# Second token half's attention transposes, value products and projection moved behind the first expert queries

## The chip, the cores and the metric

The kernel runs on one core of a Trainium2 chip. Its time is the device time of one execution in microseconds (us); the profile is one execution, taken by the hardware profiler. Engines: PE (TensorE), DVE (VectorE), ACT (ScalarE), POOL (GpSimd) and SP, which only issues transfers.

## The reference, cut to what matters

Two transformer blocks run one after the other on 256 tokens of width 1024, in float32. The change touches the second block: an attention of 8 heads beside a long convolution, both gated, merged and projected, and then a retrieval layer ("peer"), in which each token picks 8 x 16 rows out of two tables of 16384 rows.

```python
    merged = (jax.nn.sigmoid(g_attn) * (attn @ p["w_attn_out"])
              + jax.nn.sigmoid(g_hy) * (hy @ p["w_hy_out"]))
    return merged @ p["w_out"], k_self, v_self
...
        x = x + g1 * out
        x = x + g2 * peer(modulate(rmsnorm(x, norm_ffn_g[i]), sh2, sc2),
                          peer_wq[i], peer_keys1[i], peer_keys2[i], peer_u[i], peer_v[i])
...
    def chunk(xc):
        q = (xc @ wq).reshape(PEER_CHUNK, PEER_HEADS, 2, half)
        s1 = jnp.einsum('chd,hnd->chn', q[:, :, 0], keys1).astype(jnp.float32)
        s2 = jnp.einsum('chd,hnd->chn', q[:, :, 1], keys2).astype(jnp.float32)
        v1, i1 = lax.top_k(s1, PEER_TOPK)
        v2, i2 = lax.top_k(s2, PEER_TOPK)
        cand = (v1[..., :, None] + v2[..., None, :]).reshape(PEER_CHUNK, PEER_HEADS, PEER_TOPK * PEER_TOPK)
...
        best, pos = lax.top_k(cand, PEER_TOPK)
        eidx = jnp.take_along_axis(cidx, pos, axis=-1)
        g = jax.nn.softmax(best, axis=-1)
        a = jnp.einsum('chkd,cd->chk', u_tab[eidx], xc)
        wgt = (jax.nn.gelu(a.astype(jnp.float32)) * g).astype(xc.dtype)
        return jnp.einsum('chk,chkd->cd', wgt, v_tab[eidx])
```

## The kernel before, in words

The instructions of every engine stand in the order in which the code lists them; there is no scheduler. Engines wait for each other on counting semaphores. The 256 tokens are two halves of 128, t = 0 and t = 1, each one token per partition.

Attention of the second block works on eight pairs of heads-and-half: pairs 0 to 3 are half 0, pairs 4 to 7 half 1. Of pair i, `score2(i)` multiplies queries and keys into two PSUM banks, DVE takes the maximum (`unit_max`), ACT the exponential (`exp_units`), DVE divides (`unit_norm`), PE transposes the probabilities (`pt2`), ACT copies the transposes out, and PE multiplies with the values (`pv2`). After pair 3 and pair 7 ACT copies a half's result into `attnT` (`pw0`, `pw1`). `mixed_half(br, t, u)` is 16 products of 128x128 of the output projection of branch br (0 attention, 1 convolution) for half t and column half u; `merge_half` on DVE multiplies it with its gate, and adds the two branches. `out_unit_rows(place2, "b", t, n)` is the projection by `w_out`, `mix_in` adds it to the residual, `pn_square` and `pn_rows` normalize it, `half_T` transposes it, and `half_out` leaves the retrieval layer's input in `actT`.

The retrieval layer: `queries(j, t)` multiplies with the j-th quarter of the query weights (64 products of 128x128; for t = 0 quarters 0 and 1 go in two parts, "a" and "b"), and `key_scores(t, j)` compares with the keys; group j covers heads 2j and 2j+1. DVE finds the best 16 of each head (`best_of`, `rows_of_table`; both for a group and one more step are `picks_of`), and writes row numbers (`rowid`, which counts `rowid_ready` up). POOL issues one indirect DMA of 128 rows x 4 KB per pick, 512 in all, in turns of 32: {u0, u1, v0, u2, v1, ...}. A u row is multiplied with the token on DVE (`dots_of`, line 2197), a v row is weighted and summed on PE (`sum_rows`, line 1044). In the text gather n is the n-th of the 512, counted from 1.

A gathered row lands in one of 28 rooms of 4 KB per partition. The first 54 gathers take rooms by the table `ROW_ORDER`, later ones the room used longest ago. A room must have been read before it is used again. Most rooms lie in weights' places that PE reads first: `room_reader` names the PSUM group after which POOL may write there. Rooms 12 to 15 come free after `queries(0, 1)` ("pq01"), 16 to 19 after "pq11", 20 to 23 after "pq21" and 24 to 27 after "pq31", the last queries. In `ROW_ORDER` of before gather 39 is the first that takes room 20, and gather 51 the first that takes room 24. POOL also waits so that no more than 6 gathers (from the 65th on 10) are under way.

## Time and profile before

| | us |
|---|---|
| median of 3 runs | 1729.56 (1727.46 to 1732.55) |
| the profiled execution, its own time | 1723.73 |
| its span, first to last instruction | 1721.9 |
| PE busy | 1456.2 (85%) |
| DVE busy | 885.1 (51%) |
| POOL busy | 503.7 (29%) |
| ACT busy | 318.5 (18%) |

The span is the time between the first and the last instruction of any engine. Times in rows count from its start. In a timeline a row merges equal instructions that follow each other; what stands in brackets is how long the engine was idle before it, and what ended that ("issue": nothing that the profile shows). The first gather is issued at 949.18 us, so the retrieval layer's gathers fill the last 45% of the span.

### The profile page before, as it was taken

The numbers are of one execution on the slowest core, as the hardware profiler recorded it, in microseconds if no ns is written. First come the engines' busy times: TensorE is split into PE (matmuls) and PEld (weight loads), VectorE is DVE, ScalarE is ACT, GpSimd is POOL, SyncE is SP. The second block draws the span as 40 slices with busy tenths as digits, with TensorE's granted clock in tenths as the row PEclk, the third lists the DMA queues.
The fourth block names the chain that finished last, engine by engine and source line by source line (L and its number), as shares of the span: only waits on it lengthen the run. The fifth ranks groups of instructions, "written<-read, shape, count | busy, mean of one in ns | idle before, by whom it ended". The sixth has DMA issues, their size and how long they took to land.

```text
span 1721.9 us, 18101 instructions
## 1 busy us (share of the span) xinstructions
PE 1456.2 (85%) x6206; PEld 804.7 (47%) x6206; DVE 885.1 (51%) x1997; ACT 318.5 (18%) x643; POOL 503.7 (29%) x541
## 2 busy tenths in 40 slices
PE   7989989999999999999999874767767685867566
PEld 6866564444443434478878663222323232322222
DVE  3975152323232323465453988492938385744744
ACT  3124231101010101301052113111202021210001
POOL 3000000000000000000000555666666757575773
PEclk9999999999999999999999986787878788888789
DMA  9779729999999999943340978999999999999996
GB/s 314 277 278 337 293 99 382 427 428 429 429 428 429 429 428 428 381 147 125 120 135 1 343 295 317 360 394 379 350 409 330 404 340 391 337 392 349 379 370 251
DMA packets 135357, 565.40 MB, mean 328 GB/s; under 512 B 11513, under 2 KB 17446, under 8 KB 122748
## 3 DMA queue, kind: packets, MB, share of 16 engines
q1 hardware_dynamic: 60668, 295.66, 43.2%
q0 software_dynamic: 74416, 268.84, 40.8%
q8 instruction: 33, 0.54, 0.1%
q14 instruction: 32, 0.26, 0.0%
q10 hardware_dynamic: 208, 0.09, 0.0%
HBM read 563.49 MB, written 1.06 MB: 328 GB/s over the span
## 4 chain that ended last, share of the span: by engine, by line
PE 76%; issue 11%; DMA 5%; DVE 4%; POOL 3%; ACT 1%; another core or an unknown queue 0%; SPq 0%; POOLq 0%; DVEq 0%; ACTq 0%
PE psum L413 52%; PE psum L1044 22%; DMA ring<-in_peer_v_dram,attnT 2%; POOL ring L1194 2%; DVE arena L1645 1%; DMA ring<-in_peer_u_dram,attnT 1%; DMA ring<-in_w_in_dram 1%; PE psum L898 0%; DMA tok<-in_peer_v_dram,attnT 0%; PE psum L768 0%; PE psum L774 0%; DMA dft<-in_peer_v_dram,attnT 0%; POOL tok L1194 0%; DVE spec L1654 0%; PE psum L662 0%
## 5 line engine op out<-in xcount | busy, mean ns | idle before, releaser
L1044 PE MATMUL psum<-ring,arena 128*128 128x512 f32 x772 | 384.1, 647 | 180.3 <-DMA ring<-in_peer_v_dram,attnT 106.1
L1044 PEld LDWEIGHTS psum<-ring,arena 128*128 128x128 f32 x772 | 156.8, 206 | 404.7 <-issue 323.2
L413 PE MATMUL psum<-ring,arena 128*64 128x512 f32 (+1 forms) x1552 | 340.4, 594 | 1.4 <-DVE arena L1885 1.4
L2197 DVE CUSTOM_DVE_ANT_0 scratch<-ring,psum 128x1024 f32<-128x1024 f32 x216 | 255.5, 1219 | 68.6 <-DMA ring<-in_peer_u_dram,attnT 57.9
L413 PE MATMUL psum<-actT,ring 128*128 128x256 f32 (+1 forms) x1424 | 268.1, 349 | 21.6 <-issue 19.8
L1194 POOL DMA_INDIRECT dft<-in_peer_u_dram,attnT x10 | 9.9, 990 | 938.8 <-DVE attnT L2167 934.0
L413 PEld LDWEIGHTS psum<-actT,ring 128*128 128x128 f32 x1424 | 237.6, 197 | 52.3 <-issue 29.3
L1194 POOL DMA_INDIRECT ring<-in_peer_u_dram,attnT x216 | 205.9, 953 | 161.0 <-issue 63.9
L1194 POOL DMA_INDIRECT ring<-in_peer_v_dram,attnT x218 | 209.5, 961 | 70.1 <-issue 61.9
L413 PEld LDWEIGHTS psum<-ring,arena 128*64 128x64 f32 (+1 forms) x1552 | 109.2, 137 | 217.2 <-issue 203.8
L1495 ACT ACTIVATE arena<-ident,attnT 128x128 f32<-128x128 f32 x226 | 81.8, 396 | 412.5 <-PE psum L1044 183.6
L1927 DVE TENSOR_TENSOR arena<-arena,psum 128x512 f32<-128x512 f32 x16 | 16.9, 1058 | 203.9 <-PE psum L413 203.9
L413 PEld LDWEIGHTS psum<-arena,scratch 128*128 128x128 f32 x544 | 63.3, 192 | 13.3 <-issue 13.3
L413 PE MATMUL psum<-arena,scratch 128*128 128x128 f32 x544 | 67.8, 278 | 0.0
L413 PE MATMUL psum<-tok,arena 128*128 128x512 f32 x128 | 59.2, 605 | 0.0
L413 PE MATMUL psum<-ring,tok 128*128 128x512 f32 x128 | 55.8, 594 | 1.6 <-DVE tok L1753 1.6
L1951 DVE TENSOR_TENSOR resid<-resid,psum 128x512 f32<-128x512 f32 x64 | 44.0, 687 | 13.9 <-PE psum L413 13.9
L2230 DVE SCALAR_TENSOR_TENSOR scratch<-ring,attnT,scratch 128x1024 f32<-128x1024 f32 x24 | 30.8, 1285 | 37.9 <-DMA ring<-in_peer_v_dram,attnT 22.8
L1945 DVE COPY tok<-psum 128x512 f32<-128x512 f32 x16 | 11.1, 692 | 72.9 <-PE psum L413 72.9
L1645 DVE SCALAR_TENSOR_TENSOR arena<-arena,colsB 128x256 f32<-128x256 f32 x120 | 47.7, 480 | 0.0
L2122 DVE MAX8 qT<-arena 128x8 f32<-128x128 f32 x64 | 16.7, 288 | 57.4 <-remote 36.3
L1388 ACT ACTIVATE arena<-psum 128x512 f32<-128x512 f32 x16 | 9.6, 597 | 182.8 <-PE psum L413 182.8
(404 smaller groups left out, 1368.3 us busy)
## 6 DMA issues: line engine op xcount, KB each, us to landing
ring<-in_w_gate_dram SPq DMA_DIRECT2D x32, 2048.0 KB, 12.3
ring<-in_w_up_dram SPq DMA_DIRECT2D x32, 2048.0 KB, 16.5
ring<-in_w_down_dram SPq DMA_DIRECT2D x32, 2048.0 KB, 13.7
ring<-in_w_in_dram SPq DMA_DIRECT2D x15, 2048.0 KB, 14.7
ring<-in_ada_w_dram SPq DMA_DIRECT2D x12, 2048.0 KB, 11.7
ring<-in_w_out_dram SPq DMA_DIRECT2D x4, 2048.0 KB, 9.0
ring<-in_peer_wq_dram SPq DMA_DIRECT2D x4, 2048.0 KB, 15.1
ring<-in_w_attn_out_dram SPq DMA_DIRECT2D x2, 2048.0 KB, 11.8
```

The source lines that it names most:

```text
L413: return nc.tensor.matmul(o, lhsT, rhs, start=(k == 0), stop=(k == n - 1))
L1044: last = nc.tensor.matmul(psum[:, 4 + 2 * t + n, :], diag[:, i, :], rowbufs[b][:, n * 512:(n + 1) * 512], start=first, stop=final)
L1194: pool.indirect_dma_start(out=rowbufs[b], out_offset=None, in_=tab, in_offset=bass.IndirectOffsetOnAxis(ap=rowid[:, j // 4, k:k + 1], axis ...
L1388: nc.scalar.activation(silu, psum[0:BOTH, 3, :], ACT.Silu).then_inc(ev("silu_ready"), 1)
L1495: nc.scalar.activation(diag[:, i, :], ident[:, :], ACT.Identity, scale=gates[:, j // 4, k:k + 1]).then_inc(ev("diag_ready"), 1)
L1645: V.scalar_tensor_tensor(yT[:, c, :], vpad[:, c, j:j + T], w, yT[:, c, :], ALU.mult, ALU.add).then_inc(ev("tap"), 1)
L1927: V.tensor_tensor(hperm, silu.rearrange("p (q k) -> p q k", k=4), psum[0:BOTH, 4, :].rearrange("p (q k) -> p q k", k=4), ALU.mult).then_in ...
L1945: V.tensor_copy(yrow[:, 512:1024], psum[0:BOTH, 6, :]).then_inc(ev("y_ready1"), 1)
L1951: V.tensor_tensor(r, r, psum[:, MIX_BANK[n, t], :], ALU.add).then_inc(ev("mixed"), 1)
L2122: step(V.max(vals[:, 8 * r:8 * r + 8], src))
L2197: V.tensor_tensor_reduce(dotjunk[:, i % junk, :], rowbufs[b], x, 1.0, 0.0, ALU.mult, ALU.add, dots[:, t, k:k + 1]).then_inc(ev("dotted"), 1)
L2230: V.scalar_tensor_tensor(acc, rowbufs[b], w, acc, ALU.mult, ALU.add).then_inc(ev("added"), 1)
```

## The change

In the eight-pair loop only half 0 is finished. Scores and softmax of pairs 6 and 7 are placed around the attention projection of half 0, and `pt2`, `pv2` of pairs 4 to 7 and both attention projections of half 1 (`mixed_half(0, 1, 0)` and `(0, 1, 1)`) now stand behind `queries(0, 0, "a")`. The convolution's projection of half 1, which was spread over the loop, takes the place that the attention's had. Probabilities get a room for each pair instead of four in turn. The output projection of half 1 stands behind all queries of groups 0 and 1 of half 0, and on DVE `picks_of(1)` before `mix_in(1, 0)`. Rooms 2 to 5 and 6 to 9 trade their places in memory, and the table of rooms is a new one; gather 43 is now the first that takes room 20, and gather 51 still the first that takes room 24.

PE, from the end of the attention loop to the output projection of half 0. L898 are the probabilities' transposes, `scratch,vtok` the value products, `kdup,qT` the scores, `attnT,ring` the attention projection, `ring,tok` the output projection. Before:

```order
L898 MATMUL psum<-ident,arena 128x128 x8
L413 MATMUL psum<-scratch,vtok 64x128 x8
L413 MATMUL psum<-kdup,qT 128x512 x2
L898 MATMUL psum<-ident,arena 128x128 x8
L413 MATMUL psum<-scratch,vtok 64x128 x8
L413 MATMUL psum<-attnT,ring 128x128 x16
L898 MATMUL psum<-ident,arena 128x128 x8
L413 MATMUL psum<-scratch,vtok 64x128 x8
L413 MATMUL psum<-attnT,ring 128x128 x16
L898 MATMUL psum<-ident,arena 128x128 x8
L413 MATMUL psum<-scratch,vtok 64x128 x16
L413 MATMUL psum<-ring,tok 128x512 x16
```

The same place in the changed kernel, from the last transposes of half 0 on:

```order
L899 MATMUL psum<-ident,arena 128x128 x8
L414 MATMUL psum<-scratch,vtok 64x128 x16
L414 MATMUL psum<-kdup,qT 128x512 x2
L414 MATMUL psum<-attnT,ring 128x128 x32
L414 MATMUL psum<-kdup,qT 128x512 x2
L414 MATMUL psum<-ring,tok 128x512 x16
L414 MATMUL psum<-arena,ring 128x128 x16
L962 MATMUL psum<-ident,arena 128x128 x16
L422 MATMUL psum<-ident,scratch 128x128 x8
```

The transposes and value products of half 1 are gone from here; two scores stand between and behind the projections.

PE, behind the first key scores (`spec,arena`; `actT,ring` are queries, `arena,ring` the convolution's projection). Before:

```order
L413 MATMUL psum<-spec,arena 128x128 x2
L413 MATMUL psum<-actT,ring 128x128 x16
L413 MATMUL psum<-arena,ring 128x128 x16
L413 MATMUL psum<-spec,arena 128x128 x2
L413 MATMUL psum<-actT,ring 128x128 x16
L413 MATMUL psum<-ring,tok 128x512 x16
L413 MATMUL psum<-actT,ring 128x128 x16
L413 MATMUL psum<-spec,arena 128x128 x4
L421 MATMUL psum<-ident,scratch 128x128 x8
L413 MATMUL psum<-actT,ring 128x128 x32
```

The changed kernel, from the second query part on (eight transposes stand ahead of it):

```order
L414 MATMUL psum<-actT,ring 128x128 x16
L414 MATMUL psum<-scratch,vtok 64x128 x8
L899 MATMUL psum<-ident,arena 128x128 x8
L414 MATMUL psum<-spec,arena 128x128 x2
L414 MATMUL psum<-scratch,vtok 64x128 x8
L899 MATMUL psum<-ident,arena 128x128 x8
L414 MATMUL psum<-scratch,vtok 64x128 x8
L899 MATMUL psum<-ident,arena 128x128 x8
L414 MATMUL psum<-scratch,vtok 64x128 x8
L414 MATMUL psum<-attnT,ring 128x128 x32
L414 MATMUL psum<-actT,ring 128x128 x32
L414 MATMUL psum<-spec,arena 128x128 x4
```

The output projection of half 1 and its transposes now come behind these rows, and nothing stands between them.

POOL, gathers 15 to 23 of before. `tok` are rooms 10 and 11, `dotted` counts rows that DVE has read, `row_in` rows that have landed, and `bank_full` a PSUM bank that PE has filled, here "bx11" (the output projection of half 1) and "pq01":

```order
L1194 DMA tok<-in_peer_u_dram,attnT 128x1024 [waits row_in8,bank_full6]
L1194 DMA tok<-in_peer_u_dram,attnT 128x1024 [waits row_in9]
L1194 DMA ring<-in_peer_u_dram,attnT 128x1024 [waits row_in0,dotted,rowid_ready]
L1194 DMA ring<-in_peer_u_dram,attnT 128x1024 [waits row_in1,dotted]
L1194 DMA ring<-in_peer_u_dram,attnT 128x1024 [waits row_in2,dotted]
L1194 DMA ring<-in_peer_u_dram,attnT 128x1024 [waits row_in3,dotted]
L1194 DMA ring<-in_peer_u_dram,attnT 128x1024 [waits row_in10,bank_full5]
```

Gathers 17 to 23 of the changed kernel, where bank 3 is that of "bx11":

```order
L1200 DMA ring<-in_peer_u_dram,attnT 128x1024 [waits row_in0,dotted,rowid_ready]
L1200 DMA tok<-in_peer_u_dram,attnT 128x1024 [waits row_in1,bank_full3]
L1200 DMA tok<-in_peer_u_dram,attnT 128x1024 [waits row_in2]
L1200 DMA ring<-in_peer_u_dram,attnT 128x1024 [waits row_in3,dotted]
L1200 DMA ring<-in_peer_u_dram,attnT 128x1024 [waits row_in4,dotted]
L1200 DMA ring<-in_peer_u_dram,attnT 128x1024 [waits row_in5,dotted]
L1200 DMA ring<-in_peer_u_dram,attnT 128x1024 [waits row_in6,bank_full5]
```

The wait for "bx11" moved from gather 15 to gather 18, and that for "pq01" from gather 21 to gather 23.

```diff
@@ -198,7 +198,9 @@
...
-prob2 = arena2[:, 2048:4096].rearrange("p (u c) -> p u c", c=512)
+prob_rooms = [arena2[:, 0:1024], arena2[:, 1024:2048], arena2[:, 2048:3072], arena2[:, 3072:4096],
+          arena1[:, 3072:4096], arena2[:, 1024:2048], arena2[:, 2048:3072], arena2[:, 3072:4096]]
+prob2 = [room[:, 512 * r:512 * (r + 1)] for room in prob_rooms for r in range(2)]
...
@@ -217,25 +219,24 @@
...
-vflat = vtok[:, :, :].rearrange("p c t -> p (c t)")
...
-wi = vflat[:, 0:256].bitcast(U32).rearrange("p (t n) -> p t n", t=NT)
-wf = vflat[:, 256:512].rearrange("p (t n) -> p t n", t=NT)
+wi = rel[:, 0:64].bitcast(U32).rearrange("p (t n) -> p t n", t=NT)
+wf = rel[:, 64:128].rearrange("p (t n) -> p t n", t=NT)
...
-rowbufs += [ring[:, 4, r * D:(r + 1) * D] for r in range(4)] + [ring[:, 0, r * D:(r + 1) * D] for r in range(4)]
+rowbufs += [ring[:, 0, r * D:(r + 1) * D] for r in range(4)] + [ring[:, 4, r * D:(r + 1) * D] for r in range(4)]
...
-ROW_ORDER = [*range(10), *range(4), 10, 11, *range(4, 8), *range(12, 20), *range(8, 12), *range(0, 6), *range(20, 24), *range(6, 10), *range(12, 16), *range(24, 28)]
+ROW_ORDER = [*range(10), *range(7), 10, 11, *range(7, 10), *range(12, 20), *range(7), 10, 11, *range(7, 10), *range(20, 24), *range(12, 16), *range(24, 28)]
...
@@ -936,36 +937,32 @@
...
 mixed_half(1, 0, 1, (7,))
-for i in range(len(pairs)):
-    if i + 2 < len(pairs):
-        score2(i + 2)
+for i in range(4):
+    score2(i + 2)
     pt2(i)
...
         pv2(i - 1)
-    if i < 4:
-        mixed_half(1, 1, 0, (6,), (i,))
-    if i == 5:
-        landed(place2, "o0")
-        emptied(pe, "pw0")
-        mixed_half(0, 0, 0, (6,))
-    if i == 6:
-        mixed_half(0, 0, 1, (0,))
-pv2(len(pairs) - 1)
-everyday.append((7, 1, 2, 3, 4, 5, 6, 0))
+pv2(3)
+score2(6)
+landed(place2, "o0")
+emptied(pe, "pw0")
+mixed_half(0, 0, 0, (6,))
+mixed_half(0, 0, 1, (7,))
+score2(7)
+everyday.append((5, 4))
 pe.wait_ge(ev("bmerged"), 1)
...
 out_unit_rows(place2, "b", 0, 1)
-emptied(pe, "pw1")
-mixed_half(0, 1, 0)
+mixed_half(1, 1, 0, (6,))
 pe.wait_ge(ev("keys_in"), 32)
...
 for g in range(4):
-    b = bank(f"keyT{g}")
+    b = bank(f"keyT{g}", (3, 0, 1, 2))
     for c in range(4):
...
 half_T("pn", scratch, "pn_ready", 0)
-mixed_half(0, 1, 1)
+mixed_half(1, 1, 1, (7,))
 everyday.append((2, 3, 4, 5, 6, 7))
...
@@ -1004,15 +1001,24 @@
...
 key_scores(0, 0, "a", (0, 1), ("a",))
+pt2(4)
 queries(0, 0, "b", (2, 3))
-mixed_half(1, 1, 1)
+pv2(4)
+pt2(5)
 key_scores(0, 0, "b", (2, 3), ("b",))
+pv2(5)
+for i in (6, 7):
+    pt2(i)
+    pv2(i)
+emptied(pe, "pw1")
+mixed_half(0, 1, 0)
+mixed_half(0, 1, 1)
 queries(1, 0, "a", (0, 1))
+queries(1, 0, "b", (2, 3))
+key_scores(0, 1, need=("a", "b"))
 pe.wait_ge(ev("bmerged"), 2)
...
 out_unit_rows(place2, "b", 1, 1)
-queries(1, 0, "b", (2, 3))
-key_scores(0, 1, need=("a", "b"))
 half_T("pn", scratch, "pn_ready", 1)
...
@@ -1175,7 +1181,7 @@
...
-room_reader = {2: "bo011", 6: "bo111", 10: "bx11", 12: "pq01", 16: "pq11", 20: "pq21", 24: "pq31"}
+room_reader = {2: "bo111", 6: "bo011", 10: "bx11", 12: "pq01", 16: "pq11", 20: "pq21", 24: "pq31"}
...
@@ -1418,11 +1424,11 @@
...
-        if u >= 4:
-            full(act, f"qt{u - 4}")
+        if u >= 10:
+            full(act, f"qt{u - 8}")
...
-        last(nc.scalar.activation(prob2[:, u % 4, :], full(act, f"sc{u}"), ACT.Exp, bias=stat("nm2", 16)[:, u:u + 1], scale=HD ** -0.5,
+        last(nc.scalar.activation(prob2[u], full(act, f"sc{u}"), ACT.Exp, bias=stat("nm2", 16)[:, u:u + 1], scale=HD ** -0.5,
...
@@ -1447,15 +1453,18 @@
...
-exp_units(0)
-for i in range(HEADS):
-    if i + 1 < HEADS:
-        exp_units(i + 1)
+def prob_out(i):
...
-    if i == 4:
-        copy_out("pw0", attnT[:, :, 0:P])
-copy_out("pw1", attnT[:, :, P:T])
+
+exp_units(0)
+for i in range(4):
+    exp_units(i + 1)
+    prob_out(i)
+copy_out("pw0", attnT[:, :, 0:P])
+exp_units(5)
+exp_units(6)
+exp_units(7)
...
@@ -1500,12 +1509,17 @@
...
 scores_out(0, 0, "a", 0, 2)
+prob_out(4)
 queries_out(0, 0, "b", 2, 2)
+prob_out(5)
 scores_out(0, 0, "b", 2, 2)
+prob_out(6)
+prob_out(7)
+copy_out("pw1", attnT[:, :, P:T])
 queries_out(1, 0, "a", 0, 2)
-pn_square(1)
 queries_out(1, 0, "b", 2, 2)
 scores_out(0, 1)
+pn_square(1)
 half_out("pn", 1, modsc[:, 2, :], mod[:, 24:32, 0])
...
@@ -2083,17 +2097,19 @@
...
 merge_half(1, 0, 0)
-for i in range(HEADS):
+for i in range(4):
     unit_norm(i)
...
         merge_half(1, 0, 1)
-    if i + 2 < HEADS:
-        unit_max(i + 2)
-    if i == 3:
-        merge_half(1, 1, 0)
-    if i == 6:
-        merge_half(0, 0, 0, True)
+    unit_max(i + 2)
+unit_norm(4)
+unit_max(6)
+merge_half(0, 0, 0, True)
 merge_half(0, 0, 1, True)
+unit_norm(5)
+unit_max(7)
+unit_norm(6)
+unit_norm(7)
 dve.wait_ge(ev("g1_in"), 16)
...
@@ -2110,9 +2126,9 @@
...
 pn_rows(0)
-merge_half(0, 1, 0, True)
+merge_half(1, 1, 0)
 half_out("pn", 0, modsc[:, 2, :], mod[:, 24:32, 0])
-merge_half(0, 1, 1)
+merge_half(1, 1, 1)
 
...
@@ -2252,19 +2268,22 @@
...
 rows_of_table(0, (0,))
-merge_half(1, 1, 1, True)
 best_of(0, (1,), "0b")
...
 shift_of(0)
+full(dve, "pw1")
+dots_of(0, range(0, 3), 1)
+merge_half(0, 1, 0, True)
+merge_half(0, 1, 1, True)
+dots_of(0, range(3, 7), 1)
+picks_of(1)
 mix_in(1, 0)
-dots_of(0, range(0, 4), 1)
 mix_in(1, 1)
-dots_of(0, range(4, 5), 1)
+dots_of(0, range(7, 9), 1)
 pn_rows(1)
-dots_of(0, range(5, 8), 1)
+dots_of(0, range(9, 11), 1)
 half_out("pn", 1, modsc[:, 2, :], mod[:, 24:32, 0])
-picks_of(1)
-dots_of(0, range(8, GROUP))
+dots_of(0, range(11, GROUP))
 weigh(0)
...
```

## Rows read from the trace of the kernel before

**Rows 1.** The page, part 2: busy tenths of the DMA engines in 40 slices.

```profile
DMA  9779729999999999943340978999999999999996
```

**Rows 2.** Timeline of PE, 875 to 912: start, us, engine, line, shapes, count.

```profile
875.82 1.13 PE L413 MATMUL psum<-kdup,qT 64*128 64x512 f32 x4
...
876.88 1.09 PE L898 MATMUL psum<-ident,arena 128*128 128x128 f32 x8
...
877.81 1.06 PE L413 MATMUL psum<-arena,ring 128*128 128x128 f32 x8
...
880.88 1.09 PE L413 MATMUL psum<-scratch,vtok 128*64 128x128 f32 x16
...
898.27 3.84 PE L413 MATMUL psum<-attnT,ring 128*128 128x128 f32 x32
...
910.71 14.00 PE L413 MATMUL psum<-ring,tok 128*128 128x512 f32 x32
```

**Rows 3.** Timeline of PE, 938 to 976 us.

```profile
938.78 0.68 PE L413 MATMUL psum<-spec,arena 128*128 128x128 f32 x4
...
950.46 13.95 PE L413 MATMUL psum<-ring,tok 128*128 128x512 f32 x32
...
964.25 3.73 PE L413 MATMUL psum<-actT,ring 128*128 128x128 f32 x32
...
975.71 9.01 PE L413 MATMUL psum<-actT,ring 128*128 128x128 f32 x64 [3.92 <-issue]
```

**Rows 4.** Timeline of PE, 985 to 1047 us.

```profile
985.43 15.02 PE L413 MATMUL psum<-actT,ring 128*128 128x128 f32 x131
...
1012.79 8.19 PE L413 MATMUL psum<-actT,ring 128*128 128x128 f32 x51 [0.35 <-issue]
...
1020.82 1.06 PE L413 MATMUL psum<-spec,arena 128*128 128x128 f32 x8
...
1021.71 7.20 PE L413 MATMUL psum<-actT,ring 128*128 128x128 f32 x63
...
1038.18 8.26 PE L413 MATMUL psum<-actT,ring 128*128 128x128 f32 x58 [0.33 <-issue]
...
1046.27 4.63 PE L413 MATMUL psum<-spec,arena 128*128 128x128 f32 x40
```

**Rows 5.** Timeline of POOL: gathers 1, 25, 38, 39, 50, 51 and 92.

```profile
949.18 1.03 POOL L1194 DMA_INDIRECT dft<-in_peer_u_dram,attnT  x1 [934.03 <-DVE attnT L2167]
...
993.02 0.94 POOL L1194 DMA_INDIRECT ring<-in_peer_u_dram,attnT  x1 [3.02 <-PE psum L413]
...
1009.20 0.95 POOL L1194 DMA_INDIRECT ring<-in_peer_u_dram,attnT  x1 [0.30 <-issue]
...
1021.25 0.93 POOL L1194 DMA_INDIRECT ring<-in_peer_u_dram,attnT  x1 [11.11 <-PE psum L413]
...
1035.08 0.93 POOL L1194 DMA_INDIRECT ring<-in_peer_u_dram,attnT  x1 [0.30 <-issue]
...
1046.71 0.94 POOL L1194 DMA_INDIRECT ring<-in_peer_u_dram,attnT  x1 [10.69 <-PE psum L413]
...
1097.75 0.94 POOL L1194 DMA_INDIRECT ring<-in_peer_v_dram,attnT  x1 [0.31 <-issue]
```

**Rows 6.** Timeline of ACT, 880 to 933 us.

```profile
880.61 1.23 ACT L1234 ACTIVATE scratch<-psum 128x512 f32<-128x512 f32 x2
```

**Rows 7.** Timeline of DVE, 966 to 1093 us.

```profile
966.29 0.69 DVE L2101 TENSOR_TENSOR scratch<-spec,psum 128x512 f32<-128x512 f32 x1
...
975.65 0.49 DVE L2122 MAX8 qT<-arena 128x8 f32<-128x128 f32 x2
...
990.03 0.18 DVE L2167 CAST attnT<-attnT 128x32 int32<-128x32 f32 x1
...
1044.95 1.22 DVE L2197 CUSTOM_DVE_ANT_0 scratch<-dft,psum 128x1024 f32<-128x1024 f32 x1
...
1091.64 1.22 DVE L2197 CUSTOM_DVE_ANT_0 scratch<-ring,psum 128x1024 f32<-128x1024 f32 x1 [0.89 <-issue]
```

More of the change, by code:

```diff
@@ L897, in pt2 @@
                     for kc in range(4):
-                        last = nc.tensor.transpose(psum[:, b, kc * P:(kc + 1) * P], prob2[:, u % 4, kc * P:(kc + 1) * P], ident[:, :])
+                        last = nc.tensor.transpose(psum[:, b, kc * P:(kc + 1) * P], prob2[u][:, kc * P:(kc + 1) * P], ident[:, :])
                     last.then_inc(bank_full[b], 1)
@@ L2024, in unit_norm @@
                 for u in (2 * i, 2 * i + 1):
-                    v(V.tensor_scalar(prob2[:, u % 4, :], prob2[:, u % 4, :], stat("m2", 16)[:, u:u + 1], None, ALU.mult), "p2_ready")
+                    v(V.tensor_scalar(prob2[u], prob2[u], stat("m2", 16)[:, u:u + 1], None, ALU.mult), "p2_ready")
             half_ = lambda ap: ap.rearrange("p k c -> p (k c)")
@@ L2163, in rows_of_table @@
                 for half, op, arg in halves:
-                    v_pair(V.tensor_reduce(wf[:, half, ns], hot[half].rearrange("p (n a) -> p n a", a=PTOP), AX.X, ALU.add))
+                    v_pair(V.tensor_reduce(wf[:, half, 0:n], hot[half].rearrange("p (n a) -> p n a", a=PTOP), AX.X, ALU.add))
                 v_done()
-                v(V.scalar_tensor_tensor(rowf[:, t, ns], wf[:, 0, ns], float(PKEYS), wf[:, 1, ns], ALU.mult, ALU.add))
+                v(V.scalar_tensor_tensor(rowf[:, t, ns], wf[:, 0, 0:n], float(PKEYS), wf[:, 1, 0:n], ALU.mult, ALU.add))
                 v(V.tensor_copy(rowid[:, t, ns], rowf[:, t, ns]), "rowid_ready")
```

6 lines of the change are left out of this document (3 added, 3 removed).

## Prediction, made before the changed kernel ran

> **What bounds the kernel now.** I read the page first. Its DMA row [rows 1] shows slices of 9 tenths in most of the tail, so from the first gather on the kernel moves table rows almost without a pause, 512 gathers of 512 KB. The question is what holds POOL, which issues them. Its timeline [rows 5] has three numbers that matter. Gather 1 waits 934 us for the row numbers. Gathers 39 and 51 then wait 11.1 and 10.7 us for PE: they need rooms that the query weights occupy until PE has used them ("pq21", "pq31"). From gather 51 at 1046.7 on no wait for query weights is left. The tail behind it, 1721.9 - 1046.7 = 675.2 us, consists of turns that depend on each other (rooms, dots, sums), so I take it as rigid: it starts when gather 51 does. Not gather 1 but the last query product sets the end.
>
> That makes PE's path up to "pq31" the one to follow. PE is without a gap from 875.8 to 910.7 [rows 2], then projection, first queries, first key scores, which end at 939.3 [rows 3]; queries of half 1 start at 975.7 [rows 3], the first block of key scores of group 2 at 1020.8, and the last at 1046.3 [rows 4]. Within the last part PE stands nearly still twice: the block of 131 products ends at 1000.45 and the next dense one starts at 1012.79, and again from 1028.9 (1021.71 + 7.20) to 1038.18 [rows 4]. In both stretches gathers run in a chain (13 steps from 993.02 to 1009.20, 1.245 us each), and PE comes back 3.6 and 3.1 us after the last issue of the chain (1009.20, 1035.08) [rows 4, 5]. The trace names no cause; I call it the stall under gathers, and price it by these rows.
>
> **Step 1, the first gather.** What leaves PE's way ahead of the output projection of half 0: four `pt2` at 1.03, four `pv2` at 1.03 and the four interleaved quarters of the convolution's projection at about 1.0 each, 12.2 us [rows 2]; later both kernels have two half projections ahead of the first key scores. New waits: the second pair's transposes wait for its maximum and division, which the interleaved quarter hid (0.5), and nothing but one score pair of 1.06 covers the merge of the last projection, two DVE passes of 0.7 [rows 7] and the hand-over (0.5); with the 0.5 that before already waited gone again, the net is about 0.5. So -11.7: the first key scores end at 927.6, gather 1 goes out at 937.5. Bounds: -12.7 (no new wait) and -9 (ACT, whose copies take 1.23 for two [rows 6] and stand in one queue with the exponentials, falls behind PE's 3.1 per pair by 0.9 each).
>
> **Step 2, from there to the queries of half 1.** Before it took 975.7 - 939.3 = 36.4 us. Moved in: four `pt2` and four `pv2`, 8.2 us, and two attention half projections where one convolution half projection stood, +3.6. That is 11.8. Waits: each `pv2` needs ACT's copies of its transposes, 0.6 each after PE has filled the bank [rows 6]. Query and score products cover pair 4; pair 5 shows about 0.5, pairs 6 and 7 about 1.0 each, the copy of "pw1" 0.9, a bank that ACT must first read 0.5, the key scores of group 1 0.5: 4.4. Last, the residual and norm of half 1. Before, PE had the last query part and key scores (4.6 us) to do while DVE and ACT worked between the end of the output projection at 964.25 and 975.71 [rows 3]. Now nothing is left. From the projection's end DVE needs 1.6 for the end of `picks_of(1)` and then `mix_in` twice, four passes of 0.7 (2.9); ACT a square and a root, DVE behind it the scaling, held up by two dots of 1.22 that stand ahead [rows 7] (an estimate of 3.5 for the three); PE its transposes (0.9), and DVE two more dots and its `half_out` (3.1 past the transposes): 12.0 in place of 11.5 - 4.6, so +5.1. Sum 11.8 + 4.4 + 5.1 = 21.3. Queries of half 1 start at 975.7 - 11.7 + 21.3 = 985.3, 9.6 us later than before. Bounds: +4 (half of the waits hidden) to +13 (each copy late by another 0.5, the norm by 1).
>
> `picks_of(1)` in front of `mix_in` takes 14.6 us (975.65 to 990.2) [rows 7] and needs the key scores of group 1, at about 960; it ends at 975, just behind the output projection (973.3). It costs 1.6, counted above.
>
> **Step 3, the gathers in the meantime.** Gathers 1 to 6 go out from 937.5. Gather 7 needs "bo011", now the second attention projection at 950.6; gathers 7 to 17 follow until 964. Gather 18 needs "bx11" at 973.3, gathers 20 to 22 rooms that are read behind the norm (984), gather 23 "pq01" at 994.3 (before, gather 21 needed it). From 1002.7 ("pq11" for gather 27) they run in a chain at 1.245 us until gather 42, issued at 1021.4. So 11.7 us of head start are gone: at 1009.2 before had issued 38 gathers [rows 5], now it will be about 32.
>
> **Step 4, the stall under gathers.** PE reaches the place where it stood still before (24.7 us after the start of the queries) at 1010.0. The chain has then run for 7 us, as before (993.0 to 1000.4). I let it stand until 3.6 us after gather 42, 1025.0, and add the 8.0 us of the dense rest [rows 4]: "pq21" at 1033.0, against 1020.8, +12.2. Only eight gathers (43 to 50) follow instead of twelve, the last at 1042.0; PE would reach the second standstill at 1041.1 and leaves it at 1045.1, 4.0 instead of 9.3 us; + 8.1 gives "pq31" at 1053.2, against 1046.3: **+6.9**. Bounds of both stalls together: nothing at all (then the queries end at 1035.4 and gather 51 goes 11.3 earlier than before), and as long as before, 12.4 and 9.3 (+9.5), or 15 and 9.3 (+12.2). I take +6.9, since the coupling "until the chain ends" fits both stalls within 0.5 us.
>
> By the Trainium skill, Runtime: NRT & Kernel Launch, section Instruction fetch mechanics, the next block of instructions is fetched over a DMA queue while the present one runs, and the cost of crossing a block is mostly hidden. If PE's standstill were a fetch, that rule would leave nothing to it, and this change would then be faster, as in rival A. The trace disagrees with a hidden cost, if it is a fetch: 12.3 us [rows 4]; that it is one, no row here shows.
>
> **The other queue.** DVE's dots of turn 1 start at 1044.95, after `picks_of(2)`, which needs group 2's key scores [rows 4, 7]. With "pq21" at +12.2 they start at about 1056.7, +11.8. The last of them, 1091.64 before, frees a room for gather 92 at 1097.75 [rows 5, 7]; slack 4.9, which is 11.8 - 6.9. It is a tie, and I add 0 (bounds 0 and 3). Everything else moved is covered: `wi`/`wf` in other memory, and the rooms for probabilities, change no instruction's size. Query weights 2 and 3 are loaded behind the output projection, from about 966 and 973, on a DMA queue with few gathers, and are first read at 1002.
>
> **The sum.** -11.7 + 21.3 - 2.7 (stalls) = +6.9 on the profiled execution: 1723.7 + 6.9 = 1730.6. That execution was 5.8 below the median of the runs, so for the median 1729.56 + 6.9 = 1736.5 us. Runs differ by 5.1 us among themselves; 0.3% (5.2 us) is about what can be told from no change here.
>
> **Rivals.**
>
> A, faster: PE doesn't stand still, or little. The gathers run apart for most of the stretch from 965 to 1002, so that a backlog need not build. Then gather 51 follows POOL's own pace, and the tail starts up to 11.3 earlier: 1718 us. The same time comes out if, against [rows 5], the end follows gather 1 (-11.7). For it: the first gathers, and the DMA load, do move forward. Against it: POOL waited twice for the query weights, not for row numbers. It decides if the stalls sum to less than about 8 us (before 21.7). Chance 27%.
>
> B, no change: the stalls shrink by some 5 to 10 us more than I count, or the tail absorbs the delay in pauses of its own. 1730 us. Against it: a pause of POOL ends on a room or a row, and these move along. Chance 28%.
>
> C, slower by more: `picks_of(2)` and the dots get late by more than POOL, or PE's clock stays at its lower level after the idle 973 to 985. The 64 products after 975.71 took 9.01 us where 131 took 15.02 [rows 3, 4], which is 0.026 us more each; twice as long at that pace costs 2, the dots 3: 1742 us. Chance 12%.
>
> My forecast has 33%. Slower by over 0.3%: 33 + 12 = 45%; within 0.3%: 28%; faster: 27%. The range of 8 in 10 reaches from 1717, inside A, to 1744; that of the likeliest case alone is 1732 to 1742.
>
> **What would show it.** In the profile after: gather 1 near 937 (step 1); queries of half 1 starting near 985 with an idle PE of about 8 us before their transposes (step 2); POOL waiting at gathers 7, 18 and 23 (step 3); gather 43 near 1033 and gather 51 near 1054, each after a wait for PE, and PE thin between 1010 and 1025 (step 4); and 675 us from gather 51 to the end (rigid tail). Gather 51 before 1046.7, or a tail shorter than 670, makes the forecast wrong.

## The result, and the profile after

The changed kernel takes 1750.97 us (median of 4 runs, 1749.37 to 1757.92); the kernel before, run beside it, 1729.49. The ratio is 1.0127, 95% interval 1.0106 to 1.0147: slower by 21.5 us, where +6.9 was predicted, and outside the range. The direction was the forecast's (45%). The size is three times the forecast's, and larger than rival C's (1742).

The profiled execution is the slowest of the four (1757.92, span 1756.1). In it everything is 3.7 us late already ahead of the change: the score products that started at 875.82 before [rows 2] start at 879.56. "Net" below means with that taken off. These rows of PE answer to [rows 2, 3].

```profile
930.64 0.68 PE L414 MATMUL psum<-spec,arena 128*128 128x128 f32 x4
...
947.71 1.98 PE L414 MATMUL psum<-scratch,vtok 128*64 128x128 f32 x16 [2.90 <-ACT scratch L1240]
950.62 9.05 PE L414 MATMUL psum<-attnT,ring 128*128 128x128 f32 x64 [0.93 <-ACT attnT L1240]
959.50 7.31 PE L414 MATMUL psum<-actT,ring 128*128 128x128 f32 x64
976.32 2.05 PE L414 MATMUL psum<-spec,arena 128*128 128x128 f32 x8 [9.51 <-issue]
978.16 15.51 PE L414 MATMUL psum<-ring,tok 128*128 128x512 f32 x32
1000.22 1.97 PE L422 MATMUL psum<-ident,scratch 128*128 128x128 f32 x8 [6.55 <-DVE scratch L2124]
1004.30 9.48 PE L414 MATMUL psum<-actT,ring 128*128 128x128 f32 x64 [2.11 <-DVE actT L1606]
```

The first key scores have moved from 938.78 to 930.64, the queries of half 1 from 975.71 [rows 3] to 1004.30. Between them stand three gaps: 2.90 ahead of the last value products, 9.51 ahead of the key scores of group 1, 6.55 ahead of the norm's transposes. ACT's timeline has the reason of the second.

```profile
963.33 0.38 ACT L1240 ACTIVATE arena<-psum 128x256 f32<-128x256 f32 x1 [12.77 <-PE psum L414]
975.84 0.38 ACT L1240 ACTIVATE arena<-psum 128x256 f32<-128x256 f32 x1 [12.12 <-remote]
978.46 0.60 ACT L1240 ACTIVATE arena<-psum 128x512 f32<-128x512 f32 x1 [2.24 <-PE psum L414]
```

The first row is the copy of query part "a", due 3.4 us into the chain of gathers that starts at 959.93, and prompt. The middle row is the copy of part "b". PE had its products done at 966.81 (959.50 + 7.31), 6.9 us into the chain; ACT had nothing else to do, and yet it started 9 us later. DVE then makes its picks. They end with the projection (978.16 + 15.51 = 993.67), and `mix_in` starts behind both:

```profile
979.19 0.49 DVE L2138 MAX8 qT<-arena 128x8 f32<-128x128 f32 x2 [12.96 <-ACT arena L1240]
...
993.29 0.18 DVE L2183 CAST attnT<-attnT 128x32 int32<-128x32 f32 x1
...
993.74 0.69 DVE L2117 TENSOR_TENSOR scratch<-spec,psum 128x512 f32<-128x512 f32 x1
```

The rest of PE's path answers to [rows 4].

```profile
1014.49 15.24 PE L414 MATMUL psum<-actT,ring 128*128 128x128 f32 x135
...
1044.86 7.56 PE L414 MATMUL psum<-actT,ring 128*128 128x128 f32 x46 [0.63 <-issue]
1052.26 1.06 PE L414 MATMUL psum<-spec,arena 128*128 128x128 f32 x8
...
1064.20 10.00 PE L414 MATMUL psum<-actT,ring 128*128 128x128 f32 x62 [0.16 <-issue]
1074.03 4.63 PE L414 MATMUL psum<-spec,arena 128*128 128x128 f32 x40
```

And POOL, gathers 1, 7, 17, 18, 42, 43, 50 and 51, to [rows 5].

```profile
941.05 1.03 POOL L1200 DMA_INDIRECT dft<-in_peer_u_dram,attnT  x1 [925.77 <-DVE attnT L2183]
...
959.93 0.94 POOL L1200 DMA_INDIRECT ring<-in_peer_u_dram,attnT  x1 [11.47 <-PE psum L414]
...
972.42 0.94 POOL L1200 DMA_INDIRECT ring<-in_peer_u_dram,attnT  x1 [0.30 <-DMA idft<-in_peer_u_dram,attnT]
993.94 0.94 POOL L1200 DMA_INDIRECT tok<-in_peer_u_dram,attnT  x1 [20.58 <-PE psum L414]
...
1042.03 0.94 POOL L1200 DMA_INDIRECT ring<-in_peer_u_dram,attnT  x1 [1.43 <-issue]
1052.69 0.95 POOL L1200 DMA_INDIRECT ring<-in_peer_u_dram,attnT  x1 [9.73 <-PE psum L414]
...
1061.42 0.95 POOL L1200 DMA_INDIRECT ring<-in_peer_u_dram,attnT  x1 [0.30 <-issue]
1074.47 0.94 POOL L1200 DMA_INDIRECT ring<-in_peer_u_dram,attnT  x1 [12.09 <-PE psum L414]
```

Gather 1 is 8.1 us earlier than before, gather 7 3.0 later, gather 18 16.6 later, gather 51 27.8 later; the span is 34.2 longer. Gathers 7 to 17 leave in a chain from 959.93 to 972.42, and ACT's late copy comes 3.4 us after the last of them. After its chains before, PE came back in 3.6 and 3.1 us [rows 4, 5]. In the two repeats of the changed kernel, and with the norm first on DVE (below), the copy comes 3.3 to 3.5 us after gather 17.

### The profile page after: what moved, and what is told of

Read it like the earlier page. It is cut to its first block and busy times, and to the rows that moved or that the text cites. A ratio compares the mean times of both kernels' runs of the same rounds, so it can differ in the third digit from the quotient of the medians.

```text
span 1756.1 us, 18101 instructions
## 1 busy us (share of the span) xinstructions
PE 1464.6 (83%) x6206; PEld 812.5 (46%) x6206; DVE 884.1 (50%) x1997; ACT 317.9 (18%) x643; POOL 502.4 (29%) x541
## 5 line engine op out<-in xcount | busy, mean ns | idle before, releaser
L1050 PE MATMUL psum<-ring,arena 128*128 128x512 f32 x780 | 388.7, 645 | 214.1 <-DMA ring<-in_peer_v_dram,attnT 106.1
L414 PE MATMUL psum<-actT,ring 128*128 128x256 f32 (+1 forms) x1424 | 272.2, 353 | 17.5 <-issue 13.8
L414 PEld LDWEIGHTS psum<-actT,ring 128*128 128x128 f32 x1424 | 241.3, 200 | 48.5 <-issue 24.7
L1659 DVE SCALAR_TENSOR_TENSOR arena<-arena,colsB 128x256 f32<-128x256 f32 x120 | 47.7, 485 | 0.0
L1240 ACT ACTIVATE arena<-psum 128x512 f32<-128x512 f32 (+1 forms) x33 | 18.4, 559 | 149.0 <-PE psum L414 98.6
```

The source lines that it names most:

```text
L414: return nc.tensor.matmul(o, lhsT, rhs, start=(k == 0), stop=(k == n - 1))
L1050: last = nc.tensor.matmul(psum[:, 4 + 2 * t + n, :], diag[:, i, :], rowbufs[b][:, n * 512:(n + 1) * 512], start=first, stop=final)
L1240: last(nc.scalar.activation(dst, full(act, name)[:, 0:w], func, **kw), name)
L1659: V.scalar_tensor_tensor(yT[:, c, :], vpad[:, c, j:j + T], w, yT[:, c, :], ALU.mult, ALU.add).then_inc(ev("tap"), 1)
```

## The experiments

Each ratio is against the kernel before, run beside it. The kernels ran in groups, each group on one chip. The groups fall into two kinds. In kind 1 the kernel before takes 1724 to 1729 us, as above; in kind 2 1650. In kind 2 PE does not stand still under the gathers, and 384 gathers from the 65th on take 494.4 us (the kernel with both waits out) where the kernel before took 548.5 in kind 1.

Versions of the kernel before agree in both kinds up to the queries of half 1. Versions of the changed one do not: PE's gap ahead of the last value products is 2.7 to 2.9 us in all six of kind 1 and 1.03 in all six of kind 2, and with gather 7 held the queries of half 1 start at 1001.2 in kind 1 and at 990.9 in kind 2. So a ratio of one kind says little of the other. The changed kernel itself ran in kind 1 only, where its two repeats gave 1.0128 and 1.0116; that it loses in kind 2 too is not shown. "Before, again" is 3.2 us late as a whole, from the first key scores on at the latest.

The table has all profiled runs (us; "tail" is the span less the issue of gather 51).

| kernel | kind | ratio (95%) | queries half 1 | gather 51 | tail |
|---|---|---|---|---|---|
| before (the profile ahead) | 1 | 1 | 975.7 | 1046.7 | 675.2 |
| before, again | 1 | 0.9989 (0.9974-1.0004) | 979.3 | 1051.4 | 676.2 |
| changed | 1 | 1.0127 (1.0106-1.0147) | 1004.3 | 1074.5 | 681.6 |
| changed, again | 1 | 1.0128 (1.0108-1.0149) | 1005.7 | 1076.1 | 679.4 |
| changed, third | 1 | 1.0116 (1.0099-1.0133) | 1001.6 | 1069.9 | 672.1 |
| changed, norm first on DVE | 1 | 1.0148 (1.0123-1.0172) | 1004.5 | 1076.3 | 675.7 |
| changed, gather 7 held | 1 | 1.0116 (1.0099-1.0133) | 1001.2 | 1070.9 | 673.6 |
| changed, order of before | 1 | 1.0003 (0.999-1.0015) | 981.8 | 1049.4 | 671.5 |
| before, u1 dots early | 1 | 1.0042 (1.0025-1.0058) | 975.3 | 1026.1 | 701.2 |
| before, two pauses | 1 | 0.9957 (0.9938-0.9976) | 975.5 | 1039.4 | 671.9 |
| changed, order of before | 2 | 0.9998 (0.9986-1.001) | 979.4 | 1027.2 | 618.9 |
| changed, both waits out | 2 | 1.0025 (1.0015-1.0036) | 982.9 | 1031.8 | 618.7 |
| changed, gather 7 held | 2 | 1.0079 (1.0063-1.0095) | 990.9 | 1039.7 | 619.0 |
| changed, PE's order of before | 2 | 1.0117 (1.01-1.0134) | 1000.2 | 1049.0 | 619.8 |
| changed, order of before, three pauses | 2 | 1.0015 (1.0003-1.0027) | 984.6 | 1035.8 | 618.5 |
| the same, again | 2 | 1.0015 (1.0003-1.0027) | 979.5 | 1031.5 | 619.4 |
| before, gather 1 held | 2 | 1.0049 (1.0036-1.0062) | 983.8 | 1034.7 | 619.3 |
| before, three pauses | 2 | 1.0032 (1.0021-1.0044) | 975.2 | 1032.0 | 618.5 |
| the same, again | 2 | 1.0019 (1.0007-1.0031) | 975.4 | 1032.2 | 618.7 |
| before, 3 gathers under way | 2 | 1.0192 (1.0176-1.0208) | 975.4 | 1052.1 | 626.6 |

In kind 2 the tail is 618.5 to 619.8 in all kernels but the last, while gather 51 moves by 22 us: the end follows gather 51, whatever is ahead of it. In kind 1 it is 671.5 to 681.6 but for one kernel. What gather 51 waits for can differ: with the order of before in kind 2 it goes out with an idle time of 0.34 us ahead of it, and no wait for PE.

**Both orders back.** The changed kernel, with before's order around the output projection of half 1 on three engines; the rest of the change stays.

```diff
             queries(1, 0, "a", (0, 1))
-            queries(1, 0, "b", (2, 3))
-            key_scores(0, 1, need=("a", "b"))
             pe.wait_ge(ev("bmerged"), 2)
             out_unit_rows(place2, "b", 1, 0)
             out_unit_rows(place2, "b", 1, 1)
+            queries(1, 0, "b", (2, 3))
+            key_scores(0, 1, need=("a", "b"))
...
             queries_out(1, 0, "a", 0, 2)
+            pn_square(1)
             queries_out(1, 0, "b", 2, 2)
             scores_out(0, 1)
-            pn_square(1)
...
-            picks_of(1)
             mix_in(1, 0)
...
             half_out("pn", 1, modsc[:, 2, :], mod[:, 24:32, 0])
+            picks_of(1)
```

> The changed kernel, with the order around the output projection of half 1 as in the kernel before: on PE the projection in front of the second query part and the key scores of group 1, on DVE mix_in, the norm and half_out in front of picks_of(1), on ACT the square in front of the second query part's copy. Theory: the missing cover and the stalled copy cost together about 17 us; queries of half 1 should start some 15 to 18 us earlier than in the changed kernel and the time be 1733 to 1738, above the kernel before by the uncovered waits of the attention's second half. Rival (the attention work moved behind the queries is itself what costs, or the new table of rooms): 1747 or more.

> The changed kernel with the order of before around the output projection of the second half: TensorE does it between the two parts of the second product-key queries, ScalarE's square pass stands between the two copies, VectorE mixes and norms the half before it makes its picks. All the rest of the change stays. Theory (the loss sits in the lost cover: the hand-off of query part b falls under the chained gathers with nothing behind it on TensorE, and the norm then waits behind the picks): queries of the second half start by 985, gather 51 by 1055, time 1729 to 1738. Rival (the loss sits in TensorE's own standstill or in the later value products, whatever the order): still 1745 to 1752.

Measured 0.9998 in kind 2 and 1.0003 in kind 1, where the changed kernel itself took 1.0116 in the same group: the whole loss goes with the order. I had expected 1733 to 1738 us, 1.002 to 1.005 of before; it came out better. In kind 1:

```profile
958.65 13.90 PE L414 MATMUL psum<-ring,tok 128*128 128x512 f32 x32
972.39 3.73 PE L414 MATMUL psum<-actT,ring 128*128 128x128 f32 x32
976.88 1.13 PE L414 MATMUL psum<-spec,arena 128*128 128x128 f32 x8 [0.76 <-issue]
...
981.78 7.38 PE L414 MATMUL psum<-actT,ring 128*128 128x128 f32 x64 [2.90 <-DVE actT L1606]
```

The chain of gathers runs here too (7 to 17, 955.5 to 968.4), but PE is in its projection, which takes 13.90 us as in kind 2, and ACT's copy is due only at 976, when the chain is over. Nor is there a gain: gather 1 goes out at 936.91, 12 us earlier than before [rows 5], and gather 51 at 1049.4, where PE's last queries let it.

**The copy out of the gathers' way.** GpSimd waits ahead of gather 7 until ACT has copied part "b".

```diff
+                    if turn * GROUP + i == 6:
+                        emptied(pool, "pq10b")
```

> The changed kernel with one more wait: POOL issues gather 7 only when ACT has copied out the second part of group 1's queries. Theory: in the changed kernel ACT's copy of that part came about 9 us after PE had filled the bank, because the chain of gathers 7 to 17 (959.9 to 972.4) slowed ACT, as chains slowed PE later; PE then stood idle for 9.51 us. With the chain held back the copy should follow the products within 1 us, the output projection of half 1 start some 8 to 9 us earlier, gather 51 too, and the time fall from 1751 to about 1742, although gather 7 goes out later. Rival: the copy was late for another reason (an order on ACT), or the end follows the early gathers; then the time stays at 1751 or rises by the 7 us that gather 7 is late.

> The changed kernel in which GpSimd holds gather 7 until ScalarE has copied query part b, so that no gather is under way at that hand-off. Theory (ScalarE's copy came late only because of the chained gathers 7 to 17): the 9.5 us gap of TensorE ahead of the key scores goes to 2 or less, the output projection ends by 984, but the norm still waits for the picks, so queries at 991 to 996 and gather 51 some 8 to 12 us earlier than in the changed kernel, time 1739 to 1745. Rival (the gap has another cause, and the order of gathers has no part in it): the gap stays, time 1751 or more.

In kind 1 the gap ahead of the key scores goes: 0.58, where the changed kernel of the same group has 9.31. So it was the gathers that made ACT's copy late; whether they held ACT itself or PE's signal to it, the trace does not say. It brings no time, 1.0116 as the changed kernel beside it:

```profile
964.81 1.13 PE L414 MATMUL psum<-spec,arena 128*128 128x128 f32 x8 [0.58 <-issue]
965.77 13.90 PE L414 MATMUL psum<-ring,tok 128*128 128x512 f32 x32
997.12 1.97 PE L422 MATMUL psum<-ident,scratch 128*128 128x128 f32 x8 [17.45 <-DVE scratch L2126]
```

DVE has the reason:

```profile
970.38 1.22 DVE L2215 CUSTOM_DVE_ANT_0 scratch<-ring,psum 128x1024 f32<-128x1024 f32 x1 [7.99 <-DMA ring<-in_peer_u_dram,attnT]
...
971.70 0.49 DVE L2140 MAX8 qT<-arena 128x8 f32<-128x128 f32 x2
...
990.20 0.18 DVE L2185 CAST attnT<-attnT 128x32 int32<-128x32 f32 x1
```

The projection ends at 979.7, 11.3 us ahead of the changed kernel's of this group, and PE then waits 17.45 for DVE. DVE's dots ahead of the picks want gather 7, the held one (8.0 us), and the picks, 14.6 us elsewhere, take 18.9 there, with waits of their own under the same chain. The 8.0 are the experiment's own doing: without them alone the picks would end at about 982.6 (an estimate, 990.6 - 8.0), near the projection. In kind 2, under the same chain of eleven gathers, the picks take 14.6 us, and the ratio is 1.0079 with 7.1 us of the same own doing in it. So this run shows what made the copy late, and not what the copy costs.

**The norm ahead of the picks, on DVE alone.**

```diff
-            picks_of(1)
             mix_in(1, 0)
 ...
             half_out("pn", 1, modsc[:, 2, :], mod[:, 24:32, 0])
+            picks_of(1)
```

> The changed kernel with one part of the covering order alone: on DVE mix_in, norm and half_out of half 1 in front of picks_of(1); PE's and ACT's order as in the changed kernel. Theory: where ACT's copy is late, key scores of group 1 and with them picks_of(1) are late, and this order takes picks_of(1) out of the chain to the norm; the gain is what is left of it behind the end of the output projection: 0 to 3 us on a chip without a stall, up to 2 us with the stall seen in the changed kernel (there picks_of(1) and the projection ended within 0.1 us of each other). The rest of the gap to the full covering order stays with PE's order. Rival: DVE's order is the whole cause; then this version is as fast as the full covering order.

1.0148, no gain (the changed kernel in the same group 1.0128). The copy is late as in the changed kernel (gap 9.47), PE's projection ends at 995.2, and the queries start at 1004.47: the late copy holds them by way of PE alone.

**Both at once**, gather 8 held and the norm first, PE's order as changed.

> The changed kernel with two edits: GpSimd holds gather 8 until ScalarE has copied query part b (gather 7, which VectorE's dots ahead of the picks need, is let through), and VectorE mixes and norms the second half before its picks, as before. TensorE's order stays as changed. Theory (two waits in series made the loss: the copy caught under the gathers, and the norm behind the picks): the output projection ends by 981, queries of the second half start by 990, gather 51 by 1060, time 1729 to 1737 where the changed kernel takes 1744 to 1752. Rival (TensorE's order by itself costs the time, for no cover is left for the hand-off and the norm): queries after 998, time within 3 of the changed kernel.

It fell in kind 2: 1.0025, queries at 982.94.

```profile
958.85 1.13 PE L414 MATMUL psum<-spec,arena 128*128 128x128 f32 x8 [0.58 <-issue]
959.81 13.90 PE L414 MATMUL psum<-ring,tok 128*128 128x512 f32 x32
978.86 1.97 PE L422 MATMUL psum<-ident,scratch 128*128 128x128 f32 x8 [5.15 <-DVE scratch L2126]
982.94 9.33 PE L414 MATMUL psum<-actT,ring 128*128 128x128 f32 x64 [2.11 <-DVE actT L1608]
...
992.98 21.60 PE L414 MATMUL psum<-actT,ring 128*128 128x128 f32 x192
```

With PE's order as changed, little is lost: against "order of before" in this kind the queries are 3.6 us later, the norm without cover. The changed kernel has no run in kind 2, so how much of its own loss the two edits take away is not measured; against "gather 7 held" (1.0079) they gain 8 us at the queries.

**PE's order alone put back.**

> The changed kernel with one edit: TensorE does the output projection of the second half between the two parts of the second product-key queries, as before. ScalarE and VectorE keep the changed order. Theory (each of the two waits is enough to lose the time): the projection ends by 975, but the norm still stands behind the picks, which start with the key scores at 977 to 979 and take 14.4, so queries at 999 to 1003, time within 3 of the changed kernel. Rival (TensorE's order is the cause): queries by 988, time 1724 to 1732.

1.0117 in kind 2, queries at 1000.19: PE's projection is done by 969.0, and its transposes wait for DVE, whose picks stand ahead of the norm.

```profile
996.11 1.97 PE L422 MATMUL psum<-ident,scratch 128*128 128x128 f32 x8 [21.85 <-DVE scratch L2124]
```

The copy is prompt here (0.58 ahead of the key scores), but part "b" is multiplied only behind the projection, so the picks start at 975.1. In the changed kernel the two late things are branches, not a series, and both start at the copy of part "b": copy, key scores, projection on PE, and copy, key scores, picks on DVE. PE's branch alone holds the queries at 1004 (norm first on DVE, kind 1). DVE's branch, with the picks late for either reason, is enough too (1000.2 here).

**The kernel before, gather 1 held** until the second attention projection.

```diff
+                    if turn * GROUP + i == 0:
+                        full(pool, "bx10")
```

> The kernel before with one more wait: gather 1 is issued only when PE has finished the first half of the output projection of half 1 (bx10), about 8 us later than before. Theory: the end follows gather 51, which waits for PE's last queries, so the time stays within 3 us of 1729.5. Rival: the end follows gather 1; then about 1737.5.

Gather 1 at 958.07, ratio 1.0049, 7.5 us by the medians. I had expected no cost, and the number is the rival's (8 us); but the tail is as in the other kernels, and the way is not the rival's. PE waits 9.97 us ahead of the key scores, though this is kind 2. The cause is another than in the changed kernel: DVE's first four dots stand between the two passes of `mix_in` and wait for the late rows (5.5 us for the first), ACT's square waits for `mix_in`, and the copy of part "b" stands behind the square. In this kernel gather 1 has little room to be later, though none of its being earlier pays.

**Fewer gathers under way** (3 in place of 6 for the first 64), the kernel before.

> The kernel before with at most 3 instead of 6 of the first 64 gathers under way. Theory of the stall: engines stand nearly still while a backlog of gathers is queued, so with half of it PE's standstill of 12.3 us before pq21 and 9.3 us before pq31 should shrink to half or vanish, gather 51 go out 5 to 20 us earlier, and the time fall to 1710 to 1724, unless three are too few to keep the transfers going. Rival: the standstill has to do with the rate of the transfers, not with their number in the queue; then it stays, and the time is 1729 or a few us above.

1.0192. The gathers themselves are slow then, 1.3 to 2.6 us apart, and gather 51 goes at 1052.1. In kind 2 there is no standstill that it could cure, so what I expected of the standstill was not tested.

**Dots of turn 1 earlier, rooms in another order**, the kernel before: gather 53 is the first to need "pq21", gather 67 the first to need "pq31".

> The kernel before with the gate at gather 51 taken away: DVE takes the dots of turn 1 in front of picks_of(2), and the table of rooms sends gathers 39 to 66 to rooms that DVE has read, so that the room of pq21 is first needed at gather 53 and that of pq31 at gather 67. Theory: the waits of 11.1 and 10.7 us for PE in front of gathers 39 and 51 shrink, and since the tail follows the 65th gather the time falls by 5 to 20 us. Rival: the waits move elsewhere (v rows fill all rooms until PE is done with the queries and starts summing, or weights come late); then it stays within 5 us, or is slower.

Gather 51 goes 20.6 us earlier, and the time is 1.0042: the tail is 701.2, since the wait for "pq31" now stands behind it. What it shows of the standstill is worth more: 28 gathers in one chain (993.48 to 1027.35), and PE thin from 1000.5 to 1033.05, all that time.

```profile
985.89 14.57 PE L413 MATMUL psum<-actT,ring 128*128 128x128 f32 x129
1000.68 0.36 PE L413 MATMUL psum<-actT,ring 128*128 128x128 f32 x1 [0.22 <-issue]
...
1019.73 0.37 PE L413 MATMUL psum<-actT,ring 128*128 128x128 f32 x1 [2.43 <-issue]
...
1033.05 8.24 PE L413 MATMUL psum<-actT,ring 128*128 128x128 f32 x48 [0.35 <-issue]
```

**Pauses in the chain**, the kernel before. Gather 30 waits until PE has done half of queries 2 of half 1, gather 39 for half of queries 3 of half 0 (and, with three pauses, gather 43 for half of queries 3 of half 1).

```diff
+                    if i == 1 and (j, t) in ((2, 1), (3, 0)):
+                        last.then_inc(ev("gap"), 1)
...
+                    if turn * GROUP + i == 29:
+                        pool.wait_ge(ev("gap"), 1)
+                    if turn * GROUP + i == 38:
+                        pool.wait_ge(ev("gap"), 2)
```

> The kernel before with two pauses in the chain of gathers: gather 30 waits until TensorE has done half of the unit of queries before it would run dry (queries 2 of the second half), gather 39 until it has done half of the unit after it (queries 3 of the first half). Theory (under a chain of gathers TensorE gets no new instructions, and a pause of some 3 us lets them in): the two stretches of single products shrink from 12 and 9 us to 5 or less together beyond the pauses, gather 51 is issued at 1033 to 1042 instead of 1046.7, time 1716 to 1726. Rival (the standstill is not a matter of the chain being unbroken, or returns at once after each pause): gather 51 comes at 1047 or later, time 1730 to 1740.

0.9957 (0.9938 to 0.9976), the one kernel here that is faster than before: 1714.31 beside 1724.2, in one group of kind 1. Gather 51 came where I expected it (1033 to 1042), but the thin stretches left, which I had put at 5 us together, are 12.5.

```profile
985.96 21.61 PE L413 MATMUL psum<-actT,ring 128*128 128x128 f32 x192
1007.41 1.06 PE L413 MATMUL psum<-spec,arena 128*128 128x128 f32 x8
1008.31 4.02 PE L413 MATMUL psum<-actT,ring 128*128 128x128 f32 x32
...
1016.28 10.00 PE L413 MATMUL psum<-actT,ring 128*128 128x128 f32 x65 [1.73 <-issue]
...
1034.90 4.20 PE L413 MATMUL psum<-actT,ring 128*128 128x128 f32 x21 [0.82 <-issue]
```

```profile
998.52 0.94 POOL L1200 DMA_INDIRECT ring<-in_peer_u_dram,attnT  x1 [0.30 <-issue]
1004.28 0.94 POOL L1200 DMA_INDIRECT ring<-in_peer_u_dram,attnT  x1 [4.82 <-PE psum L413]
...
1017.95 0.95 POOL L1200 DMA_INDIRECT ring<-in_peer_u_dram,attnT  x1 [2.76 <-issue]
...
1039.38 0.95 POOL L1200 DMA_INDIRECT ring<-in_peer_u_dram,attnT  x1 [6.78 <-PE psum L413]
```

The 12.3 us of standstill [rows 4] are gone with a pause of 4.8: 192 products in 21.61 us, as in kind 2. Later stretches of 3.9 and 8.6 us are left, each under the next chain. Gather 51 goes 7.3 us earlier.

**Three pauses**, on the kernel before and on the changed one with the order of before, were to take the last stretch away. Both groups that had them were of kind 2, where there is none.

> The kernel before with three pauses: gather 30 waits for half of queries 2 of the second half, gather 39 for half of queries 3 of the first half, gather 43 for half of queries 3 of the second half. With two pauses TensorE still stood 8.4 us from 1026.5 to 1034.9. Theory (a pause of about 3 us at gather 43 lets the instructions in): gather 51 at 1034 to 1037 instead of 1039.4, time 3 to 5 us under that with two pauses (0.993 to 0.995 of before). Rival (the third pause costs what it gives): ratio 0.995 to 0.998.

> The changed kernel with the order of before around the second half's output projection, and three pauses: gather 32 waits for half of queries 2 of the second half, gather 39 for half of queries 3 of the first half, gather 45 for half of queries 3 of the second half. Theory (the change itself is worth nothing, since the gathers end up waiting for TensorE's later queries, and the pauses lift the standstill): gather 51 at 1035 to 1039, ratio 0.992 to 0.996, the same as the kernel before with pauses. Rival (the earlier first gathers do pay once the standstill is gone, since fewer gathers are then left for later): ratio under 0.991.

1.0032 and 1.0015 in the first, 1.0019 (1.0007 to 1.0031) and 1.0015 (1.0003 to 1.0027) in the second: where PE does not stand still, pauses cost 2 to 5 us. What three of them bring in kind 1 was not measured, nor whether the change is worth something there once the order and the standstill are both out of the way. An unchanged copy of before gave 0.9989 (0.9974 to 1.0004), which is how far a ratio of 1 strays.

## Why the prediction was wrong, step by step

**What bounds** was right: gather 51 starts the tail, and a gather 1 that is 12 us earlier is worth nothing (1.0003 with the order of before). The tail is less rigid in kind 1 than I took it: 681.6, 679.4 and 672.1 in the changed kernel's three profiles, for 675.2.

**Step 1** was right: the first key scores net 11.9 us earlier, predicted 11.7.

**Step 2 failed.** The queries of half 1 moved by +28.6, net +24.9, where +9.6 was predicted; 15.3 us are missing. The term that failed is a wait of PE for a copy by ACT, which the step priced at what it takes when no gathers run: "the key scores of group 1 0.5". That wait took 9.51 (9.0 of the 15.3). In the same class are the last value products (2.90 for 1.0, ACT's copy of their transposes being 1.59 <-remote) and PE's slower pace behind the gaps: 9.05 for two attention half projections, where 64 such products take 7.4, 15.51 for the projection, where it took 13.95, and 2.05 for the key scores, which before PE did in about 1.1: 1.9 + 1.6 + 1.6 + 0.9. From 950 to 1000 us the mean granted clock is 0.84, where it was 0.97 before. The chain behind the projection was well estimated, 10.6 for 12.0. That is 9.0 + 6.0 - 1.4 = 13.6 of 15.3; 1.7 I can't place. The gap and its place repeat in the two other runs of the changed kernel (9.51 and 9.31). I had seen the gathers' effect in the trace and charged it to PE alone, since only PE had work there before. The change put hand-offs on ACT, and picks on DVE, into the gathers' time, and step 3 of my own working had gathers 7 to 17 going out until 964, over the copy that I priced at 0.5.

The second error hides behind the first. I took `picks_of(1)` to end just behind the projection. It does (993.7 and 993.67), but only because both hang on the same late copy. So taking the picks alone off the norm's path brought nothing; holding gather 7 alone brought nothing either, there with 8.0 us of its own. Both at once was not measured in kind 1, so that the two together are the whole loss there is argued; that the loss is the order's is shown.

**Step 3** was right in its places: POOL waits at gathers 7, 18 and 23, and at 27, 43 and 51.

**Step 4** was right, counted from the queries: "pq21" 48.0 us later (predicted 47.7), "pq31" 21.8 behind it (20.2). PE came back 2.8 us after each chain's last issue. Over the profiles of before, changed, two pauses and dots early, PE turns thin 7.0 to 8.3 us after a chain's first gather, and is back 2.0 to 3.9 us after its last, once 5.7. One bound was added up wrongly: with no stall at all the step gives 9.6 - 21.7 = -12.1 for gather 51, not -11.3, and rival A's time moves by as little. The trace can now say more of what the standstill is not. The instruction packets of one queue, in 2 us windows of the kernel with two pauses, at 1004 and at 1020 us:

```profile
q8 instruction: 1, 0.02, 2.9%
...
q8 instruction: 1, 0.02, 3.0%
```

None comes between 1022 and 1042, though PE is thin from 1026.3 and dense again at 1034.9; and the first thin stretch, from 1012.3, begins 8 us behind a packet. The Trainium skill, Runtime: NRT & Kernel Launch, section Instruction fetch mechanics, says that blocks are fetched ahead, and that the cost of crossing one is mostly hidden. Of this queue that holds here: in the kernel with both waits out its packets come about 15 us apart, beside 192 products without a gap. So the reason that I gave for the pauses, that instructions get in during them, is not supported. It is not excluded for the first one, at whose end a packet falls (1004.0 to 1004.5). That unbroken chains of gathers go with the standstill in kind 1 is shown by its length (33 us under 28 gathers, none where a pause follows the first five). By what means they bring it on stays open. Not all work stops in such a chain: the output projection with the order of before (32 products of 512 columns) took 13.90 us in one, and DVE's dots in the kernel before ran 1.14 us apart from 990.5 to 1018.

**The sum.** +24.9 at the queries, the forecast's -2.7 for the stalls, and +0.3 and +1.6 against it in step 4, gives gather 51 net +24.1 (1074.47 - 1046.71 - 3.7), near the +21.5 of the medians. The profiled execution's span grew by more, net 30.5, the rest in its tail. Rival C named the lower clock, and priced it at 2. No rival had a hand-off that the gathers hold up.

## What to carry to other kernels

A hand-off that costs half a microsecond in a quiet stretch can cost nine under a chain of indirect DMAs, as ACT's copy did here; when a change moves work, price its waits by what runs beside them in the new place. Where two branches start at one late event, undoing either alone can show nothing; test them together before a cause is dropped. Starting the gathers 12 us earlier gained nothing here, since they end up waiting for the work that frees their rooms; a short pause in their chain gained 0.4%, in one of the two kinds. And run the changed kernel itself beside every experiment on it: without it, a run of the other kind cannot be set against the loss.
